# Layer norm's reciprocal root as one power on GpSimd, in place of ScalarE's root and VectorE's reciprocals, in a hybrid decoder layer

## The chip, the core and the metric

The kernel runs on one core of one Trainium2 chip. The metric is the device time of one execution in microseconds (us); a lower time is better. The engines are named as in the profile: PE is TensorE (PEld its weight loads), DVE is VectorE, ACT is ScalarE, POOL is GpSimd, SP is SyncE. Each has its own queue of instructions, and they meet by semaphores only.

## What is computed

One layer of a decoder, for 1024 prompt tokens and 64 sample tokens (1088 columns, T), in float32. The input is normalised and projected; four branches follow (two recurrences, a short gated convolution, and a wide depthwise convolution with a layer norm); gated sums of the four, an output projection and an MLP end it. The change touches only the layer norm of the fourth branch:

```
def layer_norm(x, g, b):
    mu = jnp.mean(xf, axis=-1, keepdims=True)
    xc = xf - mu
    y = xc * lax.rsqrt(jnp.mean(xc * xc, axis=-1, keepdims=True) + EPS)
    return y * g + b
...
glu = ad * jax.nn.sigmoid(gd)
y_d, buf_conf_new = causal_depthwise_conv(glu, buf_conf, conv_conf_w)
o_d = jax.nn.silu(layer_norm(y_d + conv_conf_b, ln_conf_g, ln_conf_b))
```

The branch is 512 channels wide.

## The kernel before, in words

Every float32 product is made of three products of PE: the weights and the activations are split into a high and a low part. For each tile of weights SP loads w_raw, ACT copies it to w_hi (rounded), POOL subtracts to w_lo (line 1505 through `split_lo`, four pieces of 256 columns), and only then does PE start the unit. There are two slots of weights, so the split of unit u+1 stands in each queue where unit u begins.

Activations lie with channels on the partitions and tokens in the columns. A projection unit has 128 output channels and runs over three groups of tokens (368, 368 and 352 columns), one PSUM bank each (`acc`). A group is two "halves" of products. When a group is done its bank is emptied by ACT (units fa, gates and others), or by a sigmoid on ACT followed by a multiplication on DVE, which then frees the bank (units qa and ga).

One list, `ITEMS`, made by `plan()`, sets the order of everything; each engine walks through the same list and issues its share of each item. So two items on different engines are ordered by semaphores alone, but on one engine strictly by the list. The layer norm's items ("ln", stage, number) are laid between the halves of the first value product ia (two units of 9 groups, halves 0 to 35) and of the first head's units qa (halves 36 to 41), fa (42 to 47) and ga (48 to 53). The places are in the list `norm`:

```
norm = [(3, "sum", 0), (12, "mean", 0), (14, "centre", 0)] + \
       [(at, "square", t) for t, at in enumerate((17, 18, 20, 21))] + \
       [(23, "sum", 1), (32, "var", 0), (33, "root", 0)] + \
       [(35 + j, "invert", j) for j in range(4)] + [(39 + t, "scale", t) for t in range(FT)] + \
       [(41 + 2 * t, "gate", t) for t in range(FT)] + [(49, "store", 0), (52, "stored", 0)]
```

An item with place i comes ahead of half i. POOL issues the split of fa's weights at half 36, that of ga's at half 42, and that of the next head's qa at half 48.

The stages: the four channel tiles of y_d (128 channels x 1088 tokens) are summed and a product with ones gives the mean on all partitions; y_d is centred; ACT squares, DVE and POOL add, a second product with ones gives the sum of squares in PSUM. "root": DVE scales it, adds EPS and writes ln_t (line 2224), then ACT takes the square root in place (line 1333). "invert": DVE's reciprocal of ln_t into ln_r, in four pieces of 272 columns (line 2230). "scale": DVE multiplies each tile of y_d by ln_r (through the helper at line 1790), and POOL multiplies by the gain and adds the bias (line 1639). "gate": ACT's sigmoid (line 1338), DVE's multiplication, and then SP stores the branch.

`mhalf` is a tile of 128 x 16 that holds -0.5. The kernel raises small tiles of mean squares to this power on POOL in its other norms (`rs<-ss,mhalf`, through the helper at line 1505).

Of the kernel before, what the change touches and what calls it, by code (L numbers as in the profile page):

```python
# [17 lines left out]
ALU = mybir.AluOpType  # L18
# [3 lines left out]
P = 128  # L22
# [5 lines left out]
T = TP + TS  # L28
# [256 lines left out]
def build(nc, a, o, scratch, decays):  # L285
    with ExitStack() as top:
# [863 lines left out]
        def _(act):  # L1150
# [151 lines left out]
            for it in ITEMS:  # L1302
                if it[0] == "half":
                    _, u, g, hf = it
                    if g == 0 and hf == 0 and u:
                        split_hi(u + 1)
                    if hf == 1:
                        evac(u, g)
                elif it[0] == "states_cd":
                    act.wait_ge(sem("ends_turned"), 1)  # L1310
                    copy(taild[:, :], pz[:, 2, :]).then_inc(sem("tails_done"), 1)
                    copy(tailc[:, :], pz[:, 3, :]).then_inc(sem("tails_done"), 1)
                elif it[0] == "pool_tap" and it[2]:
                    j = it[2]
                    w = par[:, 0, R_CDW + j:R_CDW + j + 1]
                    if j == 1:
                        act.wait_ge(sem("bufs_in"), 1)
                        act.wait_ge(sem("glu_done"), 3)
                        act.wait_ge(sem("pads_zero"), 1)
                    if j >= 3:  # L1320
                        act.wait_ge(sem("prod_used"), j - 1)
                    copy(tap_prod[:, j % 2, 0:TP], e_d[:, 0, j:j + TP], scale=w)
                    copy(tap_prod[:, j % 2, TP:T].rearrange("p (b t) -> p b t", t=LS), e_ds[:, 0, :, j:j + LS],
                         scale=w).then_inc(sem("prod_ready"), 1)
                elif it[0] == "ln":
                    _, stage, t = it
                    if stage == "square":
                        act.wait_ge(sem("ln_dve"), t + 1)
                        act.activation((ln_t, ln_r, sg_d, y_c)[t][:, :], y_d[:, t, :], ACT.Square) \
                            .then_inc(sem("ln_act"), 1)  # L1330
                    elif stage == "root":
                        act.wait_ge(sem("ln_dve"), FT + 1)
                        act.activation(ln_t[:, :], ln_t[:, :], ACT.Sqrt).then_inc(sem("ln_act"), 1)
                    elif stage == "gate":
                        act.wait_ge(sem("ln_affine"), t + 1)
                        if t >= 2:
                            act.wait_ge(sem("od_done"), t - 1)
                        act.activation((sg_d, y_c)[t % 2][:, :], y_d[:, t, :], ACT.Sigmoid) \
                            .then_inc(sem("ln_sig"), 1)
                elif it[0] == "phase":  # L1340
                    phase_end(act, "act", it[1])
                elif it[0] == "bsplit":
                    _, i, t = it
                    if i == 0:
                        act.wait_ge(sem("b_out"), H)
                        act.wait_ge(sem("b_cnew"), H)
                    else:
                        act.wait_ge(group_ready, GROUPS[BR_U[i - 1, 3] + 1])
                    act.wait_ge(sem("b_in"), 16 * FT * (i + 1))
                    copy(b_hi[:, t, :], b_raw[:, t, :]).then_inc(sem("b_hi_ready"), 1)  # L1350
                elif it[0] == "msplit":
                    k = it[1]
                    act.wait_ge(group_ready, GROUPS[GT_U[M_IT - 1, 7] + 1])
                    act.wait_ge(sem("m_gated"), merged_at(k))
                    copy(h_hi[:, k, :], merged[:, k, :]).then_inc(sem("mh_ready"), 1)
                    if k % 2:
                        copy(m_s[:, k - 1:k + 1, 0:TS], merged[:, k - 1:k + 1, TP:T])
                    if k == 5:
                        sample_low(0)
                elif it[0] == "rows":  # L1360
                    act.wait_ge(sem("row_dve"), 1)
                    act.activation(trow, frow, ACT.Abs).then_inc(sem("row_act"), 1)
                    act.wait_ge(sem("row_act"), 1)
                    act.activation(urow, trow, ACT.Exp, scale=-1.0).then_inc(sem("row_act"), 1)
                    act.wait_ge(sem("row_act"), 2)
                    act.activation(trow, urow, ACT.Ln, bias=1.0).then_inc(sem("row_act"), 1)
                elif it[0] == "rows_exps":
                    act.wait_ge(sem("row_dve"), 3)
                    act.activation(wint[:, :], trow, ACT.Exp).then_inc(sem("row_act"), 1)
                    act.activation(cdr[:, :], nlast[:, :], ACT.Exp).then_inc(sem("row_act"), 1)  # L1370
                    act.wait_ge(sem("rt_zero"), 1)
                    copy(rt[0:H, :], arow)
                    act.activation(rt[32:32 + H, :], mrow[:, :], ACT.Exp, scale=-1.0)
                    act.activation(rt[64:64 + H, :], urow, ACT.Exp).then_inc(sem("row_act"), 1)
                elif it[0] == "rec":
                    _, x, s, h = it
                    if x == "A":
                        if s == "turn":
                            act.wait_ge(sem("a_kturned"), h + 1)
                            copy(kta[:, 0:4, :], pz[:, 0, :].rearrange("p (c v) -> p c v", v=P))  # L1380
                            copy(kta[:, 4:8, :], pz[:, 1, :].rearrange("p (c v) -> p c v", v=P))
                            copy(kta[0:TS, NT, :], pz[0:TS, 2, 0:P]).then_inc(sem("a_kt"), 1)
                        elif s == "out":
                            out_evac("a", h, ota)
                    else:
                        if s == "score":
                            act.wait_ge(sem("b_decayed"), h + 1)
                            act.activation(wb[:, 0:TP], wb[:, 0:TP], ACT.Exp)
                            act.activation(wb[0:TS, TP:T], wb[0:TS, TP:T], ACT.Exp).then_inc(sem("b_exp"), 1)
                        elif s == "out":  # L1390
                            act.wait_ge(sem("b_out"), h + 1)
                            for j, (bk, nc_) in enumerate(((0, 3), (1, 3), (3, 2))):
                                act.activation(den[:, 3 * j:3 * j + nc_],
                                               pz[:, bk, 0:129 * nc_].rearrange("p (c n) -> p c n", n=129)[:, :, 128],
                                               ACT.Abs)
                            act.activation(den[0:TS, NT:NT + 1], pz[0:TS, 3, 386:387], ACT.Abs) \
                                .then_inc(sem("b_absden"), 1)
# [97 lines left out]
        def _(pool):  # L1495
# [95 lines left out]
            for it in ITEMS:  # L1591
# [40 lines left out]
                elif it[0] == "ln":  # L1632
                    _, stage, t = it
                    if stage == "sum" and t == 0:
                        pool.wait_ge(sem("conv_done"), FT)
                        tt(ln_r[:, :], y_d[:, 2, :], y_d[:, 3, :], ALU.add).then_inc(sem("ln_added"), 1)
                    elif stage == "scale":
                        pool.wait_ge(sem("ln_dve"), FT + 6 + t)
                        pool.tensor_scalar(y_d[:, t, :], y_d[:, t, :], par[:, t, R_LNG:R_LNG + 1],
                                           par[:, t, R_LNB:R_LNB + 1], ALU.mult, ALU.add) \  # L1640
                            .then_inc(sem("ln_affine"), 1)
# [138 lines left out]
        def _(dve):  # L1780
# [408 lines left out]
            for it in ITEMS:  # L2189
# [9 lines left out]
                elif it[0] == "ln":  # L2199
# [21 lines left out]
                    elif stage == "root":  # L2221
# [2 lines left out]
                            ins = dve.tensor_scalar(ln_t[:, c0:c1], pz[:, j, 0:c1 - c0], 1.0 / W, EPS, ALU.mult,  # L2224
                                                    ALU.add)
                        ins.then_inc(sem("ln_dve"), 1)
                    elif stage == "invert":
                        dve.wait_ge(sem("ln_act"), FT + 1)
                        q = slice(t * T // 4, (t + 1) * T // 4)
                        dve.reciprocal(ln_r[:, q], ln_t[:, q]).then_inc(sem("ln_dve"), 1)  # L2230
                    elif stage == "scale":
                        dve.wait_ge(sem("ln_dve"), FT + 5)
                        tt(y_d[:, t, :], y_d[:, t, :], ln_r[:, :], ALU.mult).then_inc(sem("ln_dve"), 1)
                    elif stage == "gate":
                        dve.wait_ge(sem("ln_sig"), t + 1)
                        tt(y_d[:, t, :], y_d[:, t, :], (sg_d, y_c)[t % 2][:, :], ALU.mult).then_inc(sem("od_done"), 1)
# [176 lines left out]
```

## Time and profile before

| | us |
|---|---|
| median of 3 runs | 2310.09 |
| lowest and highest | 2306.09, 2311.28 |
| the profiled execution | 2307.39 |
| its span | 2305.4 |

The span is the time from the first to the last recorded instruction; 2.0 us of the profiled execution lie around it. Busy time of an engine is the sum of its instructions without overlap. Times in timelines count from the start of the span.

### The profile page before, as it was taken

How to read it: one execution, taken by the hardware profiler on the slowest of the kernel's cores; microseconds unless marked ns; L12 is line 12 of the kernel's file. 1: busy time of each engine (PE TensorE's matmuls, PEld its weight loads, DVE VectorE, ACT ScalarE, POOL GpSimd, SP SyncE). 2: the span in 40 equal slices, each digit the busy share in tenths (PEclk: the TensorE clock that was granted, in tenths of full speed). 3: DMA queues.
4: the chain of work that ended last, by engine and by line, in shares of the span. 5: the costliest groups of instructions: out<-in, count | busy, mean ns of one | idle time of the engine just before them, and what ended most of it. 6: DMA issues, size and time to landing. Idle time of an engine off the chain costs nothing. (4 is left out here: it accounts for less than half of the span.)

```text
span 2305.4 us, 33335 instructions
## 1 busy us (share of the span) xinstructions
PE 2265.8 (98%) x13402; PEld 2146.6 (93%) x13402; DVE 914.6 (40%) x1436; ACT 556.6 (24%) x925; POOL 864.0 (37%) x901
## 2 busy tenths in 40 slices
PE   7999989999999999999999999999999999999998
PEld 7999989999999999999999999889989889898896
DVE  5489854535544443102112123463242332423324
ACT  4333231111232222121121213232212122121132
POOL 3677443333132224242242424443324233242341
PEclk9999999999999999999999999999999999999999
DMA  4211220121136666212112122201111111111112
GB/s 145 55 55 48 70 85 19 57 58 48 39 84 69 95 94 78 85 46 84 38 46 85 46 85 71 70 28 46 46 46 45 45 45 36 45 45 45 45 55 78
DMA packets 176800, 139.00 MB, mean 60 GB/s; under 512 B 14638, under 2 KB 155198, under 8 KB 176675
## 3 DMA queue, kind: packets, MB, share of 16 engines
q1 hardware_dynamic: 174197, 127.83, 22.4%
q0 software_dynamic: 2304, 8.91, 1.0%
q8 instruction: 86, 1.41, 0.3%
q10 hardware_dynamic: 182, 0.60, 0.1%
q14 instruction: 31, 0.25, 0.0%
HBM read 118.95 MB, written 18.73 MB: 60 GB/s over the span
## 5 line engine op out<-in xcount | busy, mean ns | idle before, releaser
L731 PE MATMUL acc<-h_hi,w_hi 128*128 128x368 f32 (+1 forms) x2584 | 855.6, 331 | 12.0 <-POOL w_lo L1505 10.5
L733 PE MATMUL acc<-h_hi,w_lo 128*128 128x368 f32 (+1 forms) x2584 | 848.7, 328 | 0.0
L732 PE MATMUL acc<-h_lo,w_hi 128*128 128x368 f32 (+1 forms) x2584 | 847.8, 328 | 0.0
L1505 POOL TENSOR_TENSOR w_lo<-w_raw,w_hi 128x256 fp32r<-128x256 f32 (+1 forms) x491 | 469.9, 984 | 827.6 <-ACT w_hi L1152 827.5
L731 PEld LDWEIGHTS acc<-h_hi,w_hi 128*128 128x128 f32 x2584 | 488.0, 189 | 18.6 <-POOL w_lo L1505 11.6
L732 PEld LDWEIGHTS acc<-h_lo,w_hi 128*128 128x128 f32 x2584 | 488.2, 189 | 0.3
L733 PEld LDWEIGHTS acc<-h_hi,w_lo 128*128 128x128 f32 x2584 | 487.9, 189 | 0.0
L1152 ACT ACTIVATE w_hi<-w_raw 128x1024 fp32r<-128x1024 f32 (+1 forms) x169 | 176.4, 1044 | 519.0 <-PE acc L733 439.2
L1790 DVE TENSOR_TENSOR x<-acc,x 128x512 f32<-128x512 f32 (+1 forms) x291 | 201.1, 691 | 183.1 <-PE acc L733 175.3
L731 PE MATMUL acc<-w_hi,u_hi 128*128 128x512 f32 x480 | 187.4, 390 | 0.9 <-POOL w_lo L1505 0.9
L732 PE MATMUL acc<-w_lo,u_hi 128*128 128x512 f32 x480 | 187.3, 390 | 0.0
L733 PE MATMUL acc<-w_hi,u_lo 128*128 128x512 f32 x480 | 186.9, 389 | 0.0
L1790 DVE TENSOR_TENSOR uu<-acc,ur 128x368 f32<-128x368 f32 (+1 forms) x96 | 51.5, 536 | 323.2 <-ACT ur L1441 323.2
L1790 DVE TENSOR_TENSOR gtmp<-acc,gsig 128x368 f32<-128x368 f32 (+1 forms) x72 | 38.6, 536 | 331.4 <-PE acc L733 331.4
L1505 POOL TENSOR_TENSOR u_lo<-uu,u_hi 128x368 fp32r<-128x368 f32 (+1 forms) x96 | 89.1, 928 | 207.9 <-ACT u_hi L1152 116.5
L732 PE MATMUL acc<-b_lo,w_hi 128*128 128x368 f32 (+1 forms) x384 | 125.7, 327 | 0.0
L733 PE MATMUL acc<-b_hi,w_lo 128*128 128x368 f32 (+1 forms) x384 | 125.4, 327 | 0.0
L731 PE MATMUL acc<-b_hi,w_hi 128*128 128x368 f32 (+1 forms) x384 | 125.3, 326 | 0.0
L1237 ACT ACTIVATE gsig<-acc 128x368 f32<-128x368 f32 (+1 forms) x96 | 45.3, 473 | 288.6 <-PE acc L733 288.6
L1793 DVE SCALAR_TENSOR_TENSOR pz<-e_d,par,pz 128x1024 f32<-128x1024 f32 x87 | 112.2, 1289 | 4.8 <-DVE e_c L1790 0.2
L731 PEld LDWEIGHTS acc<-w_hi,u_hi 128*128 128x128 f32 x480 | 90.2, 188 | 20.1 <-POOL w_lo L1505 1.3
L733 PEld LDWEIGHTS acc<-w_hi,u_lo 128*128 128x128 f32 x480 | 90.2, 188 | 19.0
(391 smaller groups left out, 2732.3 us busy)
## 6 DMA issues: line engine op xcount, KB each, us to landing
w_raw<-in_w_in SPq DMA_DIRECT2D x84, 512.0 KB, 3.9
w_raw<-in_w_up SPq DMA_DIRECT2D x32, 512.0 KB, 4.0
w_raw<-in_w_down SPq DMA_DIRECT2D x32, 512.0 KB, 3.7
b_raw<-branch_outputs POOLq DMA_DIRECT2D x16, 544.0 KB, 7.1
w_raw<-in_w_branch SPq DMA_DIRECT2D x16, 512.0 KB, 3.5
xin<-in_x_prompt SPq DMA_DIRECT2D x8, 512.0 KB, 8.3
x<-in_x_prompt SPq DMA_DIRECT2D x16, 256.0 KB, 5.2
w_raw<-in_w_out SPq DMA_DIRECT2D x8, 512.0 KB, 3.8
```

The source lines that it names most:

```text
L731: pe.matmul(out, lh, rh, start=first, stop=False)
L732: pe.matmul(out, lh, rl, start=False, stop=False)
L733: return pe.matmul(out, ll, rh, start=False, stop=last)
L1152: return act.activation(out, in_, ACT.Copy, **k)
L1237: act.activation(gsig[:, q % GS, c0:c1], src, ACT.Sigmoid).then_inc(acc_free[g], 1)
L1505: return pool.tensor_tensor(out, x, y, op)
L1790: return dve.tensor_tensor(out, x, y, op)
L1793: return dve.scalar_tensor_tensor(out, x, sc, y, op0, op1)
```

## The change

ScalarE no longer takes the root, and VectorE no longer takes the reciprocals. In their place GpSimd raises ln_t (the variance plus EPS) to the power of -0.5 and writes ln_r, in four pieces of 272 columns, at the places in the list where the reciprocals stood (35 to 38). The pieces wait for the variance alone; VectorE's first multiplication waits for all four.

```
--- before.py
+++ after.py
@@ -1328,9 +1328,6 @@
-                    elif stage == "root":
-                        act.wait_ge(sem("ln_dve"), FT + 1)
-                        act.activation(ln_t[:, :], ln_t[:, :], ACT.Sqrt).then_inc(sem("ln_act"), 1)
@@ -1634,8 +1631,13 @@
                         tt(ln_r[:, :], y_d[:, 2, :], y_d[:, 3, :], ALU.add).then_inc(sem("ln_added"), 1)
+                    elif stage == "invert":
+                        pool.wait_ge(sem("ln_dve"), FT + 1)
+                        q = slice(t * T // 4, (t + 1) * T // 4)
+                        tt(ln_r[:, q], ln_t[:, q], mhalf[:, 0:1].broadcast_to([P, T // 4]), ALU.pow) \
+                            .then_inc(sem("ln_power"), 1)
                     elif stage == "scale":
-                        pool.wait_ge(sem("ln_dve"), FT + 6 + t)
+                        pool.wait_ge(sem("ln_dve"), FT + 2 + t)
@@ -2224,12 +2226,8 @@
-                    elif stage == "invert":
-                        dve.wait_ge(sem("ln_act"), FT + 1)
-                        q = slice(t * T // 4, (t + 1) * T // 4)
-                        dve.reciprocal(ln_r[:, q], ln_t[:, q]).then_inc(sem("ln_dve"), 1)
                     elif stage == "scale":
-                        dve.wait_ge(sem("ln_dve"), FT + 5)
+                        dve.wait_ge(sem("ln_power"), 4)
```

## Rows read from the trace of the kernel before

**Rows 1.** The page: span, busy time and share of each engine.

```profile
span 2305.4 us, 33335 instructions
PE 2265.8 (98%) x13402; PEld 2146.6 (93%) x13402; DVE 914.6 (40%) x1436; ACT 556.6 (24%) x925; POOL 864.0 (37%) x901
```

**Rows 2.** Who waited for whom, 290 to 345: total us, times, longest.

```profile
PE acc L731 <- POOL w_lo L1505: 4.1, 1, 4.1
PE acc L731 <- DVE va L1790: 1.9, 1, 1.9
```

**Rows 3.** Timeline of PE: start, us, instruction, [idle before <- releaser].

```profile
302.85 0.33 PE L731 MATMUL acc<-h_hi,w_hi 128*128 128x368 f32 x1
...
314.73 0.33 PE L731 MATMUL acc<-h_hi,w_hi 128*128 128x368 f32 x1
...
330.84 0.67 PE L731 MATMUL acc<-h_hi,w_hi 128*128 128x368 f32 x1 [4.10 <-POOL w_lo L1505]
```

**Rows 4.** Timeline of POOL, 305 to 334.

```profile
305.62 3.01 POOL L1505 TENSOR_TENSOR w_lo<-w_raw,w_hi 128x256 fp32r<-128x256 f32 x4 [9.82 <-ACT w_hi L1152]
315.59 1.26 POOL L1639 TENSOR_SCALAR y_d<-y_d,par 128x1088 f32<-128x1088 f32 x1 [6.97 <-DVE y_d L1790]
318.09 7.89 POOL L1639 TENSOR_SCALAR y_d<-y_d,par 128x1088 f32<-128x1088 f32 x3 [1.24 <-DVE y_d L1790]
325.94 7.59 POOL L1505 TENSOR_TENSOR w_lo<-w_raw,w_hi 128x256 fp32r<-128x256 f32 x8
```

**Rows 5.** Timeline of DVE, 300 to 316.

```profile
300.66 1.42 DVE L2224 TENSOR_SCALAR ln_t<-pz 128x512 f32<-128x512 f32 x3 [1.46 <-PE pz L1035]
...
304.62 1.85 DVE L2230 RECIPROCAL ln_r<-ln_t 128x272 f32<-128x272 f32 x1 [2.06 <-ACT ln_t L1333]
...
312.31 1.85 DVE L2230 RECIPROCAL ln_r<-ln_t 128x272 f32<-128x272 f32 x1
314.20 1.29 DVE L1790 TENSOR_TENSOR y_d<-y_d,ln_r 128x1088 f32<-128x1088 f32 x1
315.41 0.53 DVE L1790 TENSOR_TENSOR proj_a<-acc,proj_a 128x368 f32<-128x368 f32 x1
```

**Rows 6.** By windows: length, busy us of each engine, PEclk, DMA share, GB/s.

```profile
330.80:332.00 1.20, 1.16 (x4) 1.16 (x5) 0.00 (x0) 0.00 (x0) 1.20 (x2) 0.50 0.10 9
...
335.00:336.00 1.00, 1.00 (x5) 1.00 (x5) 0.00 (x0) 0.00 (x0) 0.00 (x0) 0.56 1.02 418
336.00:337.00 1.00, 1.00 (x8) 1.00 (x7) 0.00 (x0) 0.00 (x0) 0.00 (x0) 1.00 1.01 418
```

**Rows 7.** Timeline of ACT around the root, and its reading of ga's first group.

```profile
302.18 1.28 ACT L1333 ACT_TABLE_LOAD   x1 [10.43 <-PE acc L733]
303.48 1.12 ACT L1333 ACTIVATE ln_t<-ln_t 128x1088 f32<-128x1088 f32 x1
...
305.56 1.28 ACT L1248 ACT_TABLE_LOAD   x1
307.06 0.48 ACT L1248 ACTIVATE proj_a<-acc 128x368 f32<-128x368 f32 x1 [0.22 <-PE acc L733]
...
337.44 0.48 ACT L1248 ACTIVATE proj_a<-acc 128x368 f32<-128x368 f32 x1 [8.74 <-PE acc L733]
```

**Rows 8.** Tile rs on POOL (min/median/max ns): 5 to 50, 700 to 900, 1480 to 1560.

```profile
L1505 POOL TENSOR_TENSOR rs<-ss,mhalf x9: 538/546/1557, 8.9 to 29.5; 128x1 f32<-128x1 f32 x8, 64x1 f32<-64x1 f32 x1
...
L1505 POOL TENSOR_TENSOR rs<-ss,mhalf x4: 1796/1802/1822, 714.0 to 880.5; 128x9 f32<-128x9 f32 x4
...
L1505 POOL TENSOR_TENSOR rs<-ss,mhalf x9: 538/544/571, 1487.2 to 1538.2; 128x1 f32<-128x1 f32 x8, 64x1 f32<-64x1 f32 x1
```

**Rows 9.** POOL's groups by form: busy us, mean ns of one, idle before.

```profile
L1505 POOL TENSOR_TENSOR h_lo<-merged,h_hi 128x272 fp32r<-128x272 f32 x20 | 18.5, 961 | 0.0
...
L1505 POOL TENSOR_TENSOR tree<-tree 128x16 f32<-128x16 f32 x4 | 0.9, 216 | 0.3
L1505 POOL TENSOR_TENSOR tree<-tree 128x8 f32<-128x8 f32 x4 | 0.8, 202 | 0.3
```

## The prediction

> **What bounds the kernel now.** I read the page first: TensorE (PE) is busy 2265.8 us of a span of 2305.4, 98%, while VectorE (DVE), ScalarE (ACT) and GpSimd (POOL) are busy 40, 24 and 37% [rows 1]. So work on those three costs nothing unless PE waits for it, and a delay of PE is not made good later: only 2305.4 - 2265.8 = 39.6 us of the whole span are PE's idle time. Then I read who waited for whom around the layer norm. There PE waits for the low half of a weight tile, w_lo, once, for 4.1 us; its only other wait is one of 1.9 us for VectorE [rows 2]. The timeline of PE places that wait: the first product of ga starts at 330.84 with 4.10 us of idle time ahead of it, so the unit fa ended at 326.74 [rows 3]. The reader should then see in POOL's timeline why: the four layer norm scalings run in POOL's queue ahead of ga's split, the last of them ends at 325.94, and the first four of the eight split pieces that follow end at 330.8 [rows 4]. The scalings wait for VectorE's multiplications, the first of which starts at 314.20, right behind the last reciprocal [rows 5]. So the chain that the change rebuilds already ends in a PE wait, with little slack: what is added to it beyond some us is added to the kernel. The granted clock shows the rest of the price of a wait: 0.50, the 1.2 GHz level, for some 5 us behind it, and back at 1.00 by 336 [rows 6], so that ga's first group costs 6.6 us (330.84 to ScalarE's reading at 337.44 [rows 7]) in place of 4.1 (eight steps of three products of 0.17 us), 2.5 us more.
>
> **What the change removes.** Between the variance (DVE's three pieces, 300.66 to 302.1) and the first multiplication at 314.20 lie now: a table load of 1.28 us and a root of 1.12 us on ScalarE, ended at 304.6 [rows 7], and four reciprocals of 1.85 us of 272 columns, between which DVE empties banks [rows 5]. That is 314.2 - 302.2 = 12.0 us, and all of it goes. So does the second table load of ScalarE at 305.56, which holds up nothing: the sigmoid behind it waits for PE anyway [rows 7]. Taking DVE's reciprocals away frees it for emptying banks sooner, but PE's run from 302.85 to 326.74 has no idle time in it [rows 3], and the 1.9 us that it waits for VectorE lie ahead of it; so I cost this at nothing, with that run as the cover.
>
> **What it adds: the price of a power.** GpSimd must now raise 1088 columns to -0.5, in four pieces of 272. The kernel already has this operation, in tiny forms. One column on 128 partitions takes 544 ns at the median, nine columns take 1802 [rows 8]. Both have 128 partitions, so columns are what is paid for. The slope is (1802 - 544) / 8 = 157 ns a column. A piece of 272 is then 0.544 + 271 x 0.1573 = 43.2 us, and four are 172.7 us. No row shows a power wider than nine columns, so this is a reach of thirty times. The bounds: from above, 1802 / 9 = 200 ns for every column, 54.5 us a piece and 217.8 in all; from below, the ordinary two-input operation of GpSimd of the same 272 columns, 0.93 to 0.96 us a piece (18.5 / 20 is 0.93) [rows 9], 3.7 to 3.8 in all. I take the slope: it comes from the same operation, and small forms of other operations show no such slope, 202 ns at 8 columns against 216 at 16 [rows 9], which is 2 ns a column. So the 157 ns belong to the power and not to small shapes. The first power of all took 1557 ns where its neighbours take 546 [rows 8]; the later ones show no such extra after hundreds of us of other work, so I add nothing for it.
>
> The Trainium skill states, in "GPSIMD Engine Reference", section 3.1, about 2.6 cycles an element for a two-input tensor_tensor on GpSimd; worked out at its 1.2 GHz that estimate is 0.6 us for 272 columns, and the power would then shorten the chain. The subtractions of this trace are near to that rule, and the power's rows are some seventy times above it, so I take it as a rule for additions only. The same page's section 4.1 says to keep elementwise work on VectorE rather than GpSimd, which speaks against the change.
>
> **Where it stands in the queues.** POOL idles for 9.82 us up to 305.62, that is from 295.8 [rows 4], so the first piece starts when the variance is there, 302.2. The order of items puts two pieces ahead of the split of fa's weights and two behind it. 302.2 + 2 x 43.2 = 388.5; fa's split, 3.0 us, ends at 391.5 (before: 308.6) [rows 4]. The other two end at 391.5 + 86.4 = 477.9. VectorE waits for all four, so its first multiplication moves from 314.20 to about 478.0, by 163.8 us. Queued behind that wait on VectorE are the emptying of qa's second and third bank; behind the scalings on POOL is ga's split; and SP's stores of the branch wait for the gated result. From the first multiplication on, the order and the rivals for each engine are as before, so the 16.64 us from it to the start of ga (314.20 to 330.84) should return, and ga starts at 494.6.
>
> **The same from PE's side.** PE finishes qa at 314.7 [rows 3] and finds no weights for fa until 391.5: a wait of 76.8. fa's first group runs, at the low clock, 6.6 us, to 398.1. Its second group needs the bank that VectorE frees only behind the first multiplication (1.21 us from start to start, 0.53 to empty [rows 5]), at 479.7: a wait of 81.6. This group again takes 6.6, the third 3.85 (as 352 columns at full speed), to 490.2, and the wait for ga's split is 4.4, where it was 4.1. Sum: 76.8 + 2.5 + 81.6 + 2.5 + 4.4 - 4.1 = 163.7, the same as from the chain. The low clock behind each wait is thus hidden in slack of the fa unit, except at ga, where it is paid as before.
>
> Behind ga, recurrence, gating and stores follow with their old distances, so I carry the full shift to the end. The profiled execution was 2307.4 us, 2.7 below the median of 2310.1, which is 0.12%. 2307.4 + 163.8 = 2471.2; on the median it is 2473.9. I say 2473.
>
> **The rivals.** *The power is not dear when wide.* If a wide power costs what a wide subtraction costs, the chain is 3.8 + 3.0 = 6.8 us in place of 12.0, the multiplication starts 5.2 us earlier, ga's weights are ready at 325.7, before fa ends at 326.74, and both the wait of 4.1 and the slow clock's 2.5 us go: 2310.1 - 6.6 = 2303.5, faster by 0.29%. This is the other side of the sign. It decides at (12.0 - 3.0) / 4 = 2.25 us a piece: below that the kernel gains, above it loses. For it speaks only that nothing wide was seen; against it the slope of 157 ns, where 6.3 would be needed. Chance 0.03, with 0.01 more for a price near the turning point and no change.
>
> *The slope flattens.* A loop that takes many columns at once might cost half a column's price in a wide form: 21.8 us a piece, 87.3 in all, shift 302.2 + 87.3 + 3.0 + 0.1 - 314.2 = 78.4, time 2388. Nothing in the rows points to it; one column and nine would have to be both remainders of such a loop. Chance 0.07.
>
> *The price is 200 ns a column*, because what nine columns cost is the average and one column is a special case: 302.2 + 217.8 + 3.0 + 0.1 - 314.2 = 208.9, time 2519. Chance 0.05.
>
> *Part of the delay is absorbed.* If the idle time of PE that is left behind this stretch were caused by things that the wait lets get ahead (weights, states, splits), up to about 15 of its 39.6 us could come back: 2459. Against it: the waits behind 345 are between steps of the recurrence and of the splits, which all move along. Chance 0.04.
>
> *The change does not do what it says*, for instance that the pieces are laid behind fa's and ga's splits so that PE isn't kept waiting: the order of items excludes it. I give it nothing.
>
> **How the numbers follow.** The forecast has 0.80. Its own spread is small: 1 ns a column is 1.1 us, and the wait pattern gives a few us either way. With the absorbed case 0.84 lie between 2440 and 2500; these ends stand for 127 and 182 ns a column, a margin that the reach from nine to 272 columns asks for. A measurement of this kernel tells 0.2% from no change, some 4.6 us. Faster by more than that has 0.03, within it 0.01, slower 0.96.
>
> **What the profile of the changed kernel would show.** Four power instructions of 128x272 on GpSimd at 43 us each, two before and two behind fa's split; PE idle around 315 to 391 and again around 398 to 479, with both waits put down to POOL's w_lo and to VectorE; the granted clock at 0.5 behind each; the first multiplication of y_d near 478; one table load fewer before the root and one fewer behind it; and from ga on the same distances as before. The prediction is wrong if a power piece is not between 35 and 50 us, if PE's waits in that stretch don't sum to about 160, or if the time behind ga is shorter than before by more than a few us.

## The result, and the profile after

The changed kernel took 2477.5 us (2475.9 to 2481.8, four runs), the kernel before 2310.0 beside it: a ratio of 1.073, with an interval of 1.0717 to 1.0744. That is 167.5 us more, where 163 were forecast.

The page of the changed kernel, cut to the same lines as [rows 1], with the slices of PE, POOL and the granted clock:

```profile
span 2480.0 us, 33332 instructions
PE 2275.9 (92%) x13402; PEld 2155.8 (87%) x13402; DVE 907.5 (37%) x1432; ACT 553.2 (22%) x922; POOL 1039.5 (42%) x905
PE   8999901199999999999999999999999999999998
...
POOL 4677499943332222242333232444342332332342
...
PEclk9999955599999999999999999999999999999999
```

A slice is 62 us. PE does next to nothing in slices six to eight, GpSimd is full there, and the granted clock stands at about half. GpSimd's busy time grew by 1039.5 - 864.0 = 175.5 us, PE's by 10 only: nearly all of the longer time is PE waiting. ScalarE has three instructions fewer (922 for 925), the root and two table loads.

The four powers, as the tile ln_r on POOL shows them (min, median, max in ns), and the timelines of POOL and of VectorE:

```profile
L1502 POOL TENSOR_TENSOR ln_r<-ln_t,mhalf x4: 43694/43700/43727, 302.8 to 436.6; 128x272 f32<-128x272 f32 x4
```

```profile
302.78 87.42 POOL L1502 TENSOR_TENSOR ln_r<-ln_t,mhalf 128x272 f32<-128x272 f32 x2 [7.87 <-DVE ln_t L2226]
390.17 2.76 POOL L1502 TENSOR_TENSOR w_lo<-w_raw,w_hi 128x256 fp32r<-128x256 f32 x4
392.88 87.36 POOL L1502 TENSOR_TENSOR ln_r<-ln_t,mhalf 128x272 f32<-128x272 f32 x2
481.68 1.25 POOL L1641 TENSOR_SCALAR y_d<-y_d,par 128x1088 f32<-128x1088 f32 x1 [1.43 <-DVE y_d L1792]
484.16 7.88 POOL L1641 TENSOR_SCALAR y_d<-y_d,par 128x1088 f32<-128x1088 f32 x3 [1.24 <-DVE y_d L1792]
492.02 7.60 POOL L1502 TENSOR_TENSOR w_lo<-w_raw,w_hi 128x256 fp32r<-128x256 f32 x8
```

```profile
308.19 0.54 DVE L1792 TENSOR_TENSOR proj_a<-acc,proj_a 128x368 f32<-128x368 f32 x1 [3.19 <-ACT proj_a L1248]
480.28 1.29 DVE L1792 TENSOR_TENSOR y_d<-y_d,ln_r 128x1088 f32<-128x1088 f32 x1 [171.55 <-POOL ln_r L1502]
481.49 0.53 DVE L1792 TENSOR_TENSOR proj_a<-acc,proj_a 128x368 f32<-128x368 f32 x1
```

Two powers, the split of fa's weights, two powers: then, 480.28 us into the span, the multiplication that stood at 314.20 [rows 5]. The emptying of qa's second bank follows it at 481.49, as the list of items says. From the scalings on, the durations are those of [rows 4] to 0.01 us. PE's side, its three long waits in the timeline:

```profile
392.98 0.68 PE L731 MATMUL acc<-h_hi,w_hi 128*128 128x368 f32 x1 [77.47 <-POOL w_lo L1502]
```

```profile
482.07 0.67 PE L731 MATMUL acc<-h_hi,w_hi 128*128 128x368 f32 x1 [82.40 <-DVE proj_a L1792]
496.91 0.43 PE L731 MATMUL acc<-h_hi,w_hi 128*128 128x368 f32 x1 [4.50 <-POOL w_lo L1502]
```

The first is for fa's weights, the second for the bank, the third for ga's weights; the last was 4.10 before [rows 3]. By windows (length, busy us of PE, PEld, DVE, ACT, POOL, granted clock, DMA share, GB/s) the clock is at its half level of 1.2 GHz in the long waits and just behind the last:

```profile
314.00:391.00 77.00, 1.50 (x10) 1.22 (x8) 0.00 (x0) 0.00 (x0) 77.00 (x4) 0.54 0.00 0
400.00:479.00 79.00, 0.00 (x0) 0.00 (x0) 0.00 (x0) 0.00 (x0) 79.00 (x2) 0.51 0.00 0
496.90:500.00 3.10, 3.09 (x11) 3.09 (x12) 0.00 (x0) 0.00 (x0) 3.10 (x5) 0.56 0.54 103
```

ScalarE reads ga's first group at 502.79, 5.88 us behind its first product; before, that took 6.60 (330.84 to 337.44, [rows 3] and [rows 7]):

```profile
502.79 0.48 ACT L1248 ACTIVATE proj_a<-acc 128x368 f32<-128x368 f32 x1 [8.01 <-PE acc L733]
```

### The profile page after: what moved, and what is told of

The parts are those of the page before. It is cut to its first block and busy times, and to the rows that moved or that the text cites. A ratio compares the mean times of both kernels' runs of the same rounds, so it can differ in the third digit from the quotient of the medians.

```text
span 2480.0 us, 33332 instructions
## 1 busy us (share of the span) xinstructions
PE 2275.9 (92%) x13402; PEld 2155.8 (87%) x13402; DVE 907.5 (37%) x1432; ACT 553.2 (22%) x922; POOL 1039.5 (42%) x905
## 5 line engine op out<-in xcount | busy, mean ns | idle before, releaser
L1502 POOL TENSOR_TENSOR ln_r<-ln_t,mhalf 128x272 f32<-128x272 f32 x4 | 174.8, 43706 | 7.9 <-DVE ln_t L2226 7.9
```

Of the source, the lines that this page charges most:

```text
L1502: return pool.tensor_tensor(out, x, y, op)
```

## The experiments

Two theories stood against each other on two questions. The price of a power: a constant cost a column, or a large fixed part of the wide form. And the way that it reaches the end: one chain up to VectorE's first multiplication, or separate waits of PE that can be taken away one by one. All the kernels below start from the changed kernel.

**Powers of 136, 12 and 1 columns.** Each of the four powers covers the first n columns of its piece only, and the other columns of ln_r are left as they were. The edit, with n as 136, 12 or 1:

```
-                        q = slice(t * T // 4, (t + 1) * T // 4)
-                        tt(ln_r[:, q], ln_t[:, q], mhalf[:, 0:1].broadcast_to([P, T // 4]), ALU.pow) \
+                        q = slice(t * T // 4, t * T // 4 + n)
+                        tt(ln_r[:, q], ln_t[:, q], mhalf[:, 0:1].broadcast_to([P, n]), ALU.pow) \
```

Expected of 136 columns:

> Each of the four powers covers 136 columns in place of 272; the other half of ln_r keeps older numbers, so half the tokens of this branch are not normalised. Theory (a fixed part and a constant price a column, all of it on the path that holds PE): the wide pieces of the changed kernel took 43.70 us, so a column costs (43.70 - 0.54) / 271 = 0.159 us and a piece of 136 costs 22.0 us; four are 88.2, the first multiplication starts near 302.5 + 88.2 + 2.8 = 393.5, 79 us later than in the kernel before, and the time is about 2389 us. Rival (a large fixed part of a wide power, columns cheap): the pieces stay above 30 us and the time above 2420.

Expected of 12 columns:

> Each power covers 12 columns only, the rest of ln_r keeps older numbers and the tokens there are not normalised. This is where the prediction put the turning point: a piece should cost 0.54 + 11 x 0.159 = 2.3 us, four 9.2, with fa's split of 2.8 about 12.0, as long as the chain of root and reciprocals before. Theory: within 2 us of the kernel before, 2310, with PE's wait of about 4 us at ga as before. Rival (GpSimd's power costs by being there: it takes VectorE's or the split's time as well): over 2315.

Expected of 1 column:

> Each power covers 1 column only, the rest of ln_r keeps older numbers. The chain is then 4 x 0.54 + 2.8 = 5.0 us in place of 12.0. Theory (the chain of the kernel before ends in PE's wait of 4.1 us and the slow clock behind it, 2.5 us): the wait at ga and the slow clock vanish, and the time is about 2303.5, faster by 0.28%. Rival (the wait ends on something else a moment later, such as ScalarE's or VectorE's emptying of banks): 2308 to 2310, with a wait that has another name.

Measured: with 136 columns 2386.4 us beside 2306.8 of the kernel before, a ratio of 1.0344 (1.0328 to 1.0360); with 12 columns 2307.5, a ratio of 1.0001 (0.9992 to 1.0010); with 1 column 2300.2, a ratio of 0.9971 (0.9961 to 0.9982). The powers of the three (tile ln_r on POOL, of the kernels with 136, 12 and 1 in turn):

```profile
L1502 POOL TENSOR_TENSOR ln_r<-ln_t,mhalf x4: 22031/22038/22067, 301.6 to 370.4; 128x136 f32<-128x136 f32 x4
```

```profile
L1502 POOL TENSOR_TENSOR ln_r<-ln_t,mhalf x4: 2274/2278/2292, 302.1 to 311.6; 128x12 f32<-128x12 f32 x4
```

```profile
L1502 POOL TENSOR_TENSOR ln_r<-ln_t,mhalf x4: 552/552/560, 301.9 to 307.5; 128x1 f32<-128x1 f32 x4
```

The price is very nearly a straight line: (2278 - 552) / 11 = 157 ns a column at the low end, (22038 - 2278) / 124 = 159 in the middle, (43700 - 22038) / 136 = 159 at the top. The rival of a large fixed part falls. The time follows: 136 columns cost 79.6 us on the chip, where 79 were expected.

The kernel with 12 columns stands at the turning point that the prediction named. Its powers take 2.28 us (2.25 was the figure), its first multiplication starts at 313.89, where it was 314.20, and PE's wait at ga is there as before, at 3.9 us (who waited for whom, PE, of the kernel with 12):

```profile
PE acc L731 <- POOL w_lo L1502: 3.9, 1, 3.9
```

The rival for this kernel, that a power on GpSimd also costs the time of its neighbours (over 2315 us), falls with its 2307.5.

With one column that wait is gone, and nothing takes its place: between 265 and 345 PE waits only 1.9 and 0.9 us, both ahead of the layer norm's end. The gain is 2306.8 - 2300.2 = 6.6 us (4.2 to 9.0 by the interval of the ratio), in agreement with the 4.1 us of wait and 2.5 us of slow clock that the prediction read out of the kernel before. ScalarE's timeline of that kernel shows both more sharply: it reads ga's first group 6.9 us earlier than in [rows 7].

```profile
330.54 0.48 ACT L1248 ACTIVATE proj_a<-acc 128x368 f32<-128x368 f32 x1 [2.31 <-PE acc L733]
```

**All four powers behind fa's split.** Only their places in the list change:

```
-           [(35 + j, "invert", j) for j in range(4)] + [(39 + t, "scale", t) for t in range(FT)] + \
+           [(37, "invert", j) for j in range(4)] + [(39 + t, "scale", t) for t in range(FT)] + \
```

> The four powers keep their 272 columns, but the first two move behind the split of fa's weights, so that all four follow it. Everything is computed. Theory (the total is set by the chain up to the first multiplication, since VectorE's emptying of qa's second bank stands behind it): PE's wait for fa's weights of 77.5 us vanishes, and the wait for VectorE behind fa's first group grows to about 160 us; the time stays at the changed kernel's 2477.5 within 4 us. Rival (the two waits of PE add up, so taking one away gives it back): about 2400.

Measured: 2475.2 us, a ratio to the kernel before of 1.0723 (1.0707 to 1.0739), against 1.073 (1.0717 to 1.0744) of the changed kernel. Who waited for whom, PE, 299 to 520, of this kernel:

```profile
PE acc L731 <- DVE proj_a L1792: 164.9, 1, 164.9
PE acc L731 <- POOL w_lo L1502: 4.5, 1, 4.5
```

The wait of 77.5 us for fa's weights is gone and the one for the bank has grown from 82.4 to 164.9. The two waits are one chain seen at two places, so taking the first away gives nothing back. fa's weights are ready 86 us sooner (306.6 in place of 392.9), which lets PE do one group of fa sooner, and no more.

**Tokens on the partitions.** If a power is paid for by columns, and every partition holds the same sum of squares (the product with ones has copied it 128 times), then the 1088 numbers should lie as eight columns of 128 and one of 64. The core of the edit:

```
-           [(35 + j, "invert", j) for j in range(4)] + ...
+           [(35, "invert", 0), (37, "spread", 0)] + ...
# PE, "var"
+                        for i, (t0, t1) in enumerate(TT_):
+                            mm = pe.matmul(pz[0:t1 - t0, 3, i:i + 1], ln_t[:, t0:t1], ones[:, 0:1], start=True,
+                                           stop=True)
# PE, "spread"
+                        pe.wait_ge(sem("ln_power"), 2)
+                        for i, (t0, t1) in enumerate(TT_):
+                            n = t1 - t0
+                            mm = pe.matmul(pz[:, t0 // 512, t0 % 512:t0 % 512 + n],
+                                           rs[0:n, i:i + 1].broadcast_to([n, P]), ident[0:n, 0:n], start=True,
+                                           stop=True)
# POOL, "invert"
+                        tt(rs[:, 0:NT], ss[:, 0:NT], mhalf[:, 0:NT], ALU.pow).then_inc(sem("ln_power"), 1)
+                        tt(rs[0:TS, NT:NT + 1], ss[0:TS, NT:NT + 1], mhalf[0:TS, NT:NT + 1], ALU.pow) \
+                            .then_inc(sem("ln_power"), 1)
# DVE, "scale"
-                        tt(y_d[:, t, :], y_d[:, t, :], ln_r[:, :], ALU.mult)
+                        tt(y_d[:, t, :], y_d[:, t, :], pz[:, 0:3, :].rearrange("p a n -> p (a n)")[:, 0:T], ALU.mult)
```

> A version made to beat both, everything computed. The sum of squares is made with tokens on the partitions (nine products of ln_t against one column of ones), GpSimd's power is taken of 128x8 and 64x1, and nine small products against the identity spread the result over all partitions into PSUM, from where VectorE's multiplications read it. Theory (a power's price goes by columns): the powers take about 0.54 + 7 x 0.159 = 1.65 and 0.54 us; the spread runs at its place in PE's queue near 305 and takes about 2.5 us, so the first multiplication starts near 307.5 in place of 314.2; PE's wait at ga and the slow clock behind it, 6.6 us together, go, against 1 to 2.5 us more of PE's own work: about 2305, faster by 0.2%. Rival (the small products cost PE more than the wait was worth, or VectorE's multiplications are slower out of PSUM and hold up the banks): 2310 or more.

Measured: 2302.3 us beside 2306.4 of the kernel before, a ratio of 0.9985 (0.9976 to 0.9994). Timelines of POOL and PE, the emptying of qa's first bank and the first multiplication on VectorE, and ga's first group on ScalarE:

```profile
300.93 2.17 POOL L1511 TENSOR_TENSOR rs<-ss,mhalf 128x8 f32<-128x8 f32 x2 [6.67 <-DVE ss L2235]
304.55 2.79 POOL L1511 TENSOR_TENSOR w_lo<-w_raw,w_hi 128x256 fp32r<-128x256 f32 x4 [1.44 <-ACT w_hi L1161]
```

```profile
298.34 2.25 PE L1035 MATMUL pz<-con,ln_t 128*128 128x1 f32 x18
304.98 2.31 PE L1042 MATMUL pz<-con,rs 128*128 128x128 f32 x18
```

```profile
310.04 0.54 DVE L1801 TENSOR_TENSOR proj_a<-acc,proj_a 128x368 f32<-128x368 f32 x1 [5.53 <-ACT proj_a L1257]
310.72 1.29 DVE L1801 TENSOR_TENSOR y_d<-y_d,pz 128x1088 f32<-128x1088 f32 x1
```

```profile
333.24 0.48 ACT L1257 ACTIVATE proj_a<-acc 128x368 f32<-128x368 f32 x1 [2.32 <-PE acc L733]
```

The two powers take 2.17 us in place of 174.8. The spread costs PE 2.31 us (each float32 product is two records, so nine are 18). PE's wait at ga and the slow clock behind it are gone, which is worth 6.6; less 2.3 that leaves 4.3, and ga's first group is read 4.2 us earlier than in [rows 7]. The medians differ by 4.1 (1.4 to 5.5 by the interval of the ratio). One expectation missed: the first multiplication did not start at 307.5 but at 310.72, behind the emptying of qa's first bank, which comes ahead of it in the list and itself comes later by PE's spread, at 310.04. It cost nothing, since ga's weights are ready by 326.6 (322.72 + 3.87), before fa's last group is read at 329.23. This version is faster than both kernels, by 0.15% against the one before.

## Why the prediction was right

**The price of the power** held: 43.7 us a piece against 43.2. The reach from nine columns to 272 was off by 1%, 159 ns a column in place of 157, and that is 4 x 0.53 = 2.1 us of the difference of 4.5 between forecast and measurement. The bound from above (54.5) and the one from below (0.96) were both far away; what had chosen between them, that the slope belongs to the operation, was right.

**The chain** held: from the variance (302.7) to the first multiplication (480.28) it is 177.6, where 478.0 - 302.2 = 175.8 was worked out: 2.1 more for the powers, 0.2 less for fa's split (2.76 for 3.0). The variance itself came 0.5 us later than was taken, behind a stretch from 296 to 299 with the granted clock at 0.50, which lies ahead of everything that the change touches. From there to ga's first product it is 496.91 - 480.28 = 16.63 us, against 16.64 before. What the prediction took as unchanged behind the multiplication was unchanged.

**PE's waits** were 77.5, 82.4 and 4.5 us, against 76.8, 81.6 and 4.4. The groups of fa between them ran from 392.98 to 399.67 (482.07 less 82.40), 6.7 us against 6.6, and from 482.07 to 492.41, 10.3 us against 10.45. The slow clock behind the first two waits was indeed hidden inside the fa unit. At ga it cost less than the prediction had put down: the group ran 5.9 us in place of 6.6. The granted clock was at 0.50 in it for 3.4 us (497.3 to 500.7), where before it was so for 5.1 (330.8 to 335.9). So the shift of 166.1 us at ga's first product is 165.4 where its first group is read. The run with all powers behind fa's split shows the same thing from the other side: PE's waits are the shadow of one chain.

**The rivals.** The one on the other side, a gain below 2.25 us a piece, had its mechanism and its turning point right: with powers of 2.28 us the kernel is level with the one before, with powers of 0.55 us it gains the 6.6 us. Only the premise, a cheap wide power, is false. The flat slope and the 200 ns a column are excluded by the straight line over four widths. As for the delay being absorbed, nothing came back: the profile shows a delay of 165.4 us at the reading of ga's first group, and the median difference is 167.5.

**What it did not see.** The two traces end 2480.0 - 2305.4 = 174.6 us apart, 9 us more than at ga, so the forecast that the shift is carried unchanged to the end did not hold for this pair of executions. The profiled execution, of 2481.8 us, is 4 us above the median of its kernel, and the one of the kernel before 3 below its own. The trace tells why only in part. From 524.6 to 528.0 the granted clock was at 0.50 once more, at a place where the kernel before ran at 1.00, which is 1.6 us. And in the stretch behind ga up to the output projection PE waited three times for split weights where the kernel before waited twice (who waited for whom, before and then after):

```profile
PE acc L731 <- POOL w_lo L1505: 5.7, 2, 3.8
```

```profile
PE acc L731 <- POOL w_lo L1502: 9.6, 3, 3.8
```

The other three runs, at 2475.9 to 2477.7, do not have those us in their times, so I take this wait as one of that execution; their traces were not taken, so this is not shown. What speaks for it is that the same stretch varies in kernels that do not differ there. Counted by the starts of the same PE instructions, 750 to 950 us into the kernel before, it is 6.8 us longer in the changed kernel, but between 2.4 shorter and 2.6 longer in the traces of the five experiments.

The Trainium skill's rule of 2.6 cycles an element on GpSimd ("GPSIMD Engine Reference", section 3.1) is given for a two-input tensor_tensor and measured there with an addition: the power's 159 ns a column is 191 cycles at the 1.2 GHz that the page states, an estimate from both. The measurement decides here. For ordinary operations the trace is near the rule only when they are wide: the addition of 128x1088 into ln_r took 2.53 us, 2.8 cycles a column by the same estimate, while the subtraction of 272 columns, 0.93 to 0.96 us [rows 9], is about 1.6 times the 0.6 us that the rule gives, further off than the prediction's "near". The advice of the Trainium skill in section 4.1 of that page, to do addition, multiplication and maximum on VectorE and not on GpSimd, does not speak of powers. The trace points the same way for this job, without comparing the same operation: the reciprocals took 1.85 us for 272 columns [rows 5], the power 43.7.

## What to carry to other kernels

Two tiny instances of an operation in a trace, of different widths, give its price by column; multiply it out before the operation is made wide, and compare it with a cheap operation of the same small shapes to see whose slope it is. An expensive operation on values that are copies over all partitions belongs into the transposed layout: 1088 powers cost 2.2 us as nine columns and 175 us as 1088, and the way back by nine small products cost 2.3. Before a wait is taken away, look which instruction stands behind which in the queues: PE's wait for weights, 77 us, was worth nothing because behind it PE waited another 82 us for a bank that the same chain held.

## What the runs showed of the hardware

GpSimd's power costs 0.55 us for one column and 0.157 to 0.159 us for each further one, on 128 partitions, over widths from 1 to 272; a subtraction of 272 columns there costs 0.96 us. It did not get cheaper with width at all, which the prediction had held possible. VectorE read its second operand of 1088 columns from three neighbouring PSUM banks in one instruction of 1.29 us, as long as the same multiplication out of SBUF (1.29 us) [rows 5].
